# Two of the eight places of the expert weights' ring given up

## The reference, cut to what matters

```
h = rmsnorm(x) * (1 + sc1) + sh1;  z = h @ w_in
x = x + gt1 * (concat(attention(z), hgrn2(z)) @ w_out)      # also writes the updated states
h = rmsnorm(x) * (1 + sc2) + sh2
logits = h @ w_router + b_router -> top 4 of 32 experts, softmax weights
for e in 32 experts:                                         # w_up[e] 1024 x 2048, w_down[e] 1024 x 1024
    y = clamped_swiglu(h @ w_up[e] + b_up[e]) @ w_down[e] + b_down[e]
    out = out + weight_of(token, e) * y
x = x + gt2 * out;  y = rmsnorm(x) * g_final
```

## Time and profile before

| | us |
|---|---|
| median of 3 runs | 1183.83 (1180.34 to 1188.38) |
| the profiled execution | 1183.96 |
| its span, first to last instruction | 1182.2 |
| PE busy in the span | 1104.1 (93%) |
| DVE / ACT / POOL busy | 350.7 / 163.6 / 56.8 |
| read from memory in the span | 460.82 MB, 395 GB/s |

### The profile page before, as it was taken

The page is one execution under the profiler, slowest core; times in us unless marked ns, Lnnn a source line. Parts: engine busy times, 40 slices in busy tenths (PEclk is TensorE's granted clock), DMA queues, the critical chain, the costliest instruction groups (busy, mean ns, idle before and its releaser), DMA issues.

```text
span 1182.2 us, 14032 instructions
## 1 busy us (share of the span) xinstructions
PE 1104.1 (93%) x5473; PEld 446.0 (38%) x5473; DVE 350.7 (30%) x752; ACT 163.6 (14%) x314; POOL 56.8 (5%) x88
## 2 busy tenths in 40 slices
PE   7999999999999999989898989898989898989896
PEld 3787756643233333322232322232323222222222
DVE  3436267242312212222212121212121212121214
ACT  2332161311010101000100010001000100000003
POOL 3120000210000000000000000000000000000000
PEclk9899999999999999999999999999999999999999
DMA  9891289999999999999999999999999999999994
GB/s 350 334 309 72 77 351 352 344 376 412 429 429 431 429 432 429 432 430 432 429 431 431 431 431 429 432 429 432 429 432 430 431 430 431 430 430 431 428 431 185
DMA packets 47096, 462.18 MB, mean 391 GB/s; under 512 B 6545, under 2 KB 9809, under 8 KB 19146
## 3 DMA queue, kind: packets, MB, share of 16 engines
q1 hardware_dynamic: 40354, 445.24, 89.8%
q0 software_dynamic: 5760, 13.65, 3.3%
q10 hardware_dynamic: 952, 2.88, 0.6%
HBM read 460.82 MB, written 5.78 MB: 395 GB/s over the span
## 4 chain that ended last, share of the span: by engine, by line
PE 56%; DMA 39%; DVE 3%; ACT 1%; issue 1%; SPq 1%; DVEq 0%
PE bank L1499 27%; DMA arena<-in_w_up 17%; DMA ring<-in_w_up 17%; PE bank L1379 6%; PE bank L1523 4%; PE bank L975 3%; DMA arena<-in_w_down 3%; PE bank L952 3%; PE bank L1292 2%; PE bank L870 2%; DMA ring<-in_w_ada 2%; PE bank L1492 2%; PE bank L1048 1%; PE bank L1032 1%; PE bank L1385 1%; PE bank L894 1%
## 5 line engine op out<-in xcount | busy, mean ns | idle before, releaser
L1499 PE MATMUL bank<-arena 128*64 128x512 f32 x1024 | 239.9, 600 | 11.9 <-DMA arena<-in_w_up 11.3
L1499 PE MATMUL bank<-ring,arena 128*64 128x512 f32 x1024 | 240.0, 601 | 11.0 <-DMA ring<-in_w_up 9.8
L1499 PEld LDWEIGHTS bank<-arena 128*64 128x64 f32 x1024 | 67.2, 136 | 164.9 <-issue 149.7
L1499 PEld LDWEIGHTS bank<-ring,arena 128*64 128x64 f32 x1024 | 66.0, 136 | 164.8 <-issue 137.6
L1523 PE MATMUL bank<-arena 128*64 128x512 f32 x512 | 114.8, 596 | 9.2 <-DMA arena<-in_w_down 9.2
L1523 PE MATMUL bank<-ring,arena 128*64 128x512 f32 x512 | 114.6, 596 | 9.0 <-DMA ring<-in_w_down 9.0
L2045 DVE TENSOR_SCALAR arena<-bank 128x256 f32<-128x256 f32 x64 | 24.2, 420 | 275.5 <-PE bank L1499 275.5
L1379 PE MATMUL bank<-arena,mods 128*128 128x512 f32 (+1 forms) x204 | 93.7, 630 | 0.9 <-DVE arena L2072 0.9
L824 ACT ACTIVATE arena<-arena 128x512 f32<-128x512 f32 x32 | 20.2, 630 | 495.0 <-DVE arena L2045 495.0
L2034 DVE TENSOR_TENSOR x<-x,bank 128x512 f32<-128x512 f32 x64 | 44.0, 688 | 145.9 <-PE bank L1379 145.9
L870 PE MATMUL bank<-const,arena 128*128 128x128 f32 (+3 forms) x348 | 50.7, 285 | 20.3 <-DMA ring<-in_w_down 7.6
(11 more groups left out here) (328 smaller groups left out, 795.2 us busy)
## 6 DMA issues: line engine op xcount, KB each, us to landing
ring<-in_w_up SPq DMA_DIRECT2D x64, 2048.0 KB, 34.1
arena<-in_w_up SPq DMA_DIRECT2D x64, 2048.0 KB, 34.3
ring<-in_w_down SPq DMA_DIRECT2D x32, 2048.0 KB, 33.6
arena<-in_w_down SPq DMA_DIRECT2D x31, 2048.0 KB, 33.4
ring<-in_w_ada SPq DMA_DIRECT2D x24, 1024.0 KB, 13.4
ring<-in_w_in SPq DMA_DIRECT2D x4, 2048.0 KB, 14.9
ring<-in_w_in SPq DMA_DIRECT2D x3, 1024.0 KB, 17.3
arena<-in_state_hgrn POOLq DMA_DIRECT2D x8, 256.0 KB, 8.4
```

Source lines behind the costliest of these rows:

```text
L1499: mm = pe.matmul(B[2 * e + c % 2][64 * a:64 * a + 64, :], lhsT=xTe[:, k, 64 * e:64 * e + 64], rhs=big(PER * s + n)[:, r, 512 * c:512 * (c ...
```

## The change

`BIGS` becomes 6: the ring of big loads has places 0 to 5 alone. The early issues of loads 6 and 7 are taken out, and with them the waits that guarded their places. Loads 6 and 7 are issued by `load_later` like all others behind them, when loads 0 and 1 are used up. Every load n now waits for load n - 6 in place of n - 8. Nothing else changes: the same 192 loads of the same size and order, the same instructions on PE, DVE, ACT and POOL (POOL still waits for its own store of the decode states). `seventh` and `eighth` keep their definitions and are used by nobody.

```diff
-BIGS = 8
+BIGS = 6
...
             for c in (4, 5):
                 expert_chunk(c, 0)
-            sp.wait_ge(sem("states_stored"), 16 * NB)
-            expert_chunk(6, 0)
             sp.wait_ge(chunks_used, PRE)
             for c in (2, 3):
                 expert_chunk(c, 0)
-            wait_emptied(sp, "rt2")
-            wait_filled(sp, "xn20")
-            wait_filled(sp, "xn21")
-            expert_chunk(7, 0)
             sp.wait_ge(sem("npass_ready"), 1)
```

## The result

The changed kernel takes 1189.42 us (median of 20 runs, 1186.32 to 1191.79) where the kernel before takes 1182.23 (20 runs, 1179.58 to 1188.38). The ratio is 1.0061, 95% interval 1.0052 to 1.0070: **7.2 us slower, 6.1 to 8.3**. The forecast said 9.7 us, 0.8%, and 1193.5 us with a range of 1188 to 1199.

What follows compares the result with a forecast made beforehand. The prediction took the weight stream, continuous from about 271 us, to bound the kernel; 1183.96 us plus 9.7 for two loads moved later, with other terms at nothing, gave 1193.7, or 1193.5 us against the median, range 1188 to 1199.

Steps and rivals of the forecast that it cites:

- The two regimes and the bound: PE sets 53.5 us a pair until about 461 us, then the continuous weight stream sets 59.2 us to the end.
- Load n is issued when load n + 2 was: First pair: load 6 gets load 8's issue time, 250.4 us, and so on; each load also lands when load n + 2 did.
- The price of 9.7 us: Stream closes up two loads later: 4.194 MB at 430.5 GB/s, 9.7 us; bounds 8.9 to 9.9 us.
- The lower bound: Loads 6 to 9 have less beside them; if the 0.8 us saved reaches load 9, the price is 8.9 us.
- The time of 1193.5 us: Profiled 1183.96 us plus 9.7 is 1193.7, less 0.1 to the median: 1193.5 us, 0.8% slower.
- faster queue: Rival: from 285 to 1160 us five transfers in flight move faster than seven, 435 GB/s, ending about 1184 us; chance 6%.
- The steady part at nothing: Two fewer transfers queued in the steady part, 4.6 to 5.3 in flight, still give the full rate: 0 us.
- Moved for nothing: Loads 6 and 7, issued at 223.6 and 239.8 us, fill time nobody else wants: 4 MiB moved for nothing.
- The cushion: After the first pair load 12 is 5.6 us ahead of PE; first weight wait near 353 us instead of 461, waits about 64 us.
- the first pair at another time than 246.5 us: Sign that the prediction is wrong: the tensor engine begins the first pair at a time other than 246.5 us.
- Dry ring: Rival: under three in flight in PE's slow first loads of each pair, 2.5 us lost in each of 15 pairs, 37 us; chance 8%.
- Hidden anyway: Rival: PE's 15.3 us cushion and stream pauses after 285 us absorb the loss, leaving 1184 us; chance 4%.

Runs made afterwards that it cites:

- clean profiles: Five of six profiles of the unchanged kernel's start, with load 12 landing 31.6 to 31.8 us after T, the moment load 0 is used up.
- unlucky profile: First profile of the unchanged kernel, on which the forecast rests; load 12 landed 34.3 us after load 0 was used up.
- three ahead: Kernel before, but from load 104 on SP stays three loads ahead of PE instead of eight: 1200.36 us, ratio 1.0155, +18.3 us.

## Why the prediction was right, and what was off in size

**The two regimes and the bound**: right. The steady GB/s are 430 and 431 in both kernels, and the loss is one shift early on, of which the stream later gives a little back (below).

**"Load n is issued when load n + 2 was", landings likewise**: right against the clean profiles. Load 10 of the changed kernel lands at T + 31.4 (271.2 + 10.2 - 250.0), load 12 of the kernel before at T + 31.7. By load 19 the shift is 75.5 - 66.05 = 9.4 us, the two loads' transfer time less 0.3. Six ahead with all early issues gives the same, which the forecast's rule (when the stream becomes continuous) demands.

**The price of 9.7 us**: right where the stream closes, too large at the end; measured 7.2. Against the clean profiles load 12 is 9.7 us later (41.4 less 31.7), load 19 is 9.4 later, and load 190 is taken up 7.6 later (917.55 less the mean 909.95 of the two). The measured 7.2, 6.1 to 8.3, agrees with 7.6 and needs nothing more. So the 9.7 lose 0.3 us up to load 19 and 1.8 on the long way from there to load 190. The lower bound's 0.8 us was real for the first loads: load 6 took 7.8 and 7.6 us where load 8 had taken 9.0 to 9.7 in the three profiles; but in the clean ones that delay is gone by load 12, so it isn't in the price.

The unlucky profile isn't what made the forecast too large: the 9.7 us are two loads' transfer time and not a position read from it. It made the marks wrong, the landings of load 12 and of all behind it. One in six profiles of that start is like it, so the typical loss may lie a little under the clean one; no run measures by how much. I had also read the 9.5 us of load 11 as those of a lone load. In that profile load 11 was issued at T + 17.8 while load 10 landed at T + 21.4, so something was left over: a delay that the clean profiles have worked off by load 12.

**The time of 1193.5 us** was 4.1 too high: 2.5 are the price, 1.6 the base, since the median of 3 runs (1183.83) stands that much above the median of 20 (1182.23). 1189.42 lies below the 1190.5 to 1196.5 that the prediction gives the forecast alone. It is inside 1188 to 1199 because the range went further down for a partial gain of the faster queue. A small gain of the stream did come, but not for that rival's reason: in this the range held partly by luck.

**"The steady part at nothing"**: the term that was mis-sized. It is right for the number in flight, which costs and brings nothing down to three. But from load 19's landing to PE taking up load 190 it is 843.0, 843.4 and 844.4 us in the three profiles of the kernel before, 842.1 and 842.0 in the changed one (917.6 - 75.5, 917.5 - 75.5), and 841.4 with four places: 1.0 to 2.4 us come back with six. Eight places with six ahead from the start have 918.9 - 75.1 = 843.8, as the others with eight places, so it isn't the number in flight. Of the 844.4, 0.9 us come at once between the landings of loads 20 and 24. The rest is spread evenly: from load 72's landing to load 180's, nine pairs, it takes 532.6 to 532.9 us in ten profiles with eight places (with three ahead left out), 532.1 in both with six, 531.8 with four. It goes with the number of places, or with which rooms they are. Why was not found; no run moved the places while keeping their number.

**"Moved for nothing", each at 4.9 us**: as a price of each early load this would have been wrong, though the forecast needed it only for both together in a ring without them. Alone, load 7 is worth 0.6 us and load 6 2.0 in time, 2.1 and 3.5 at load 12's landing, because the unfilled stretch behind T takes a part up, if there is a place to put it in. With six places there is none, and the whole price is due at load 12.

**The cushion**: PE's first wait came at 395 us, not 353. Load 12 landed at 291.3 us, not 294.4, since its forecast position was read from the unlucky profile; the cushion at 299.6 us was thus 8.3 us, and 8.3 / 5.7 = 1.5 pairs after it is 378 us. That is still 17 us before the first wait that is seen, as 444 was before 461: the sum of cushion and pace comes out early by the same amount in both kernels. So PE's waits begin later than forecast and add up to 58.9 us, not 64.

**A sign of being wrong that marks nothing**: the first pair at another time than 246.5 us. It began at 246.1 in the changed kernel, and at 246.2 and 243.3 in the other profiles of the kernel before.

**The rivals.** *Dry ring*: not at six; at three ahead, with two in flight, it costs 2.45 us a pair where I had worked out 2.5. *Hidden anyway*: no pause, as said. *Faster queue*: the stream did gain 1 to 2 us over its length, but not through fewer in flight; it needed 9.7 to reach zero. The rule of the Trainium skill ("SBUF — State Buffer", "Summary: rules for kernel authors") would make two loads 11.7 us, as an estimate from that page. The trace disagrees: both kernels hold 430 to 431 GB/s, at which two loads are 9.7 us, and the landings shift by 9.7 at load 12. Two more places given up cost 10.4 us in time, too wide a measure to tell 9.7 from 11.7, and 9.5 to 10.2 in positions.

## What to carry to other kernels

In a kernel bound by a stream of weights, a buffer more is worth what it lets the stream move before it closes up, once; after that only enough transfers in flight matter, and here three of 2 MiB were enough and two were not. Price an early transfer by the idle time it fills less the idle time that is left behind it to fill: here either of two loads alone could be late for 2.1 or 3.5 us at load 12 in place of 4.9, and both for 6.7; with no place to catch up in, for 9.7. Before a term of a few us is read from one profile, take the same landing in a second one, counted from an event close by.

## What the runs showed of the hardware that I had not expected

- A 2 MiB load with at most the last 2 us of the one ahead beside it took 7.6 to 8.0 us from issue to landing (loads 6 to 9 of the changed kernel). In the kernel before, with up to 1 MB of small transfers in the 6 us behind T, loads 8 to 11 took 7.6 to 9.9 us in its three profiles, and in one of them the delay stayed for four loads although they came only every 6 us.
- The rate held at 430 GB/s with 3.1, 5 and 7 loads of 2 MiB in flight and fell to 414 at 2.1, while the busy share of the DMA engines read 1.01 and 1.00: the share didn't show the loss, GB/s did.
- The same stream of 171 loads, from load 19's landing to load 190, took 843.0 to 844.4 us with eight places, 842.0 with six and 841.4 with four.
